# Pooling by one 144-column product per channel block, the 16 columns that reach into the next tile added by VectorE, on one TensorE-bound core

## What is computed

```python
POOL_WINDOWS = (2, 4, 8, 16)       # one for each group of 256 channels

def _pool_mixer(h_ctx, h, w_pool, pool_scale):
    he = jnp.concatenate([h_ctx, h], axis=1)
    cs = jnp.pad(jnp.cumsum(he, axis=1), ((0, 0), (1, 0), (0, 0)))
    hi = c + 1 + jnp.arange(t)
    for gi, w in enumerate(POOL_WINDOWS):
        lo = jnp.maximum(hi - w, 0)
        csg = cs[:, :, gi * 256:(gi + 1) * 256]
        mean = (csg[:, hi] - csg[:, lo]) / (hi - lo)
        ys.append(mean - h[:, :, gi * 256:(gi + 1) * 256])
    z = einsum('ntgc,gce->ntge', stack(ys), w_pool)
    return z * pool_scale
```

## Time and profile before

| | |
|---|---|
| median of three runs | 2282.36 us (2281.73 to 2285.25) |
| the profiled execution | 2281.3 us |
| its span, first to last instruction | 2279.5 us |
| PE busy in the span | 2218.8 us, 97% |
| DVE / ACT / POOL busy | 42% / 29% / 6% |
| the pooling stage, from pooling(0) to the end of the first `up_chunk` products | about 1401 to 1518 us |
| mean granted TensorE clock | 0.994 |

### The profile page before, as it was taken

One profiled execution on the slowest core, in us unless ns is written; L12 is line 12 of the kernel. 1 busy time (PEld: TensorE's weight loads), 2 busy tenths in 40 slices (PEclk: granted clock), 3 DMA queues, 4 the chain that ended last, 5 costly groups with the idle time before them and its releaser, 6 DMA issues.

```text
span 2279.5 us, 33504 instructions
## 1 busy us (share of the span) xinstructions
PE 2218.8 (97%) x13723; PEld 1996.8 (88%) x13723; DVE 961.8 (42%) x1694; ACT 658.9 (29%) x1293; POOL 137.5 (6%) x216
## 2 busy tenths in 40 slices
PE   6999999898999999999999999989999999999998
PEld 6999877686789989899898998889989899898996
DVE  4120386575643424334243345663424334243346
ACT  4111496543432203122031223451303113031121
POOL 1000130000120000000000003330000000000001
PEclk9999999999999999999999999999999999999999
DMA  5230400398321202012020123230202102021023
GB/s 167 80 86 29 158 2 2 114 404 291 102 93 46 65 10 74 27 46 64 9 74 25 49 92 110 89 102 28 66 9 74 46 28 65 9 74 45 29 90 119
DMA packets 127934, 176.15 MB, mean 77 GB/s; under 512 B 14365, under 2 KB 96469, under 8 KB 127708
## 3 DMA queue, kind: packets, MB, share of 16 engines
q1 hardware_dynamic: 121644, 170.05, 22.7%
q10 hardware_dynamic: 6192, 4.72, 0.7%
HBM read 156.40 MB, written 18.58 MB: 77 GB/s over the span
## 4 chain that ended last, share of the span: by engine, by line
PE 76%; DMA 2%; DVE 1%; SPq 1%; issue 0%; ACT 0%; POOL 0%; DVEq 0%; POOLq 0%; ACTq 0%
PE ps L1731 33%; PE ps L1711 33%; PE ps L2606 4%; DMA sa_va<-cache_a_v 1%; PE ps L2555 1%; PE ps L2574 1%; PE ps L1390 1%; PE ps L1720 1%; PE ps L1447 1%; PE ps L1410 0%; DVE m_xT_lo L2361 0%; PE ps L2626 0%; DMA sa_kb<-cache_b_k 0%; SPq L654 0%; PE ps L1430 0%
## 5 line engine op out<-in xcount | busy, mean ns | idle before, releaser
L1675 DVE TENSOR_TENSOR t_y<-t_y,ps 128x512 f32<-128x512 f32 x288 | 197.7, 687 | 626.4 <-PE ps L1731 626.2
L1731 PE MATMUL ps<-t_w_hi,t_h_hi 128*128 128x512 f32 x1152 | 449.7, 390 | 2.9 <-DVE t_h_hi L1652 2.2
L1731 PE MATMUL ps<-t_w_lo,t_h_hi 128*128 128x512 f32 x1152 | 448.4, 389 | 0.0
L1731 PE MATMUL ps<-t_w_hi,t_h_lo 128*128 128x512 f32 x1024 | 398.4, 389 | 0.0
L1711 PE MATMUL ps<-m_xT_lo,t_w_hi 128*128 128x384 f32 x1488 | 327.9, 328 | 0.0
L1711 PE MATMUL ps<-m_xT_hi,t_w_lo 128*128 128x384 f32 x1488 | 327.9, 328 | 0.0
L1711 PE MATMUL ps<-m_xT_hi,t_w_hi 128*128 128x384 f32 x1488 | 327.8, 328 | 0.0
L1606 ACT ACTIVATE t_relu<-ps 128x384 f32<-128x384 f32 (+1 forms) x192 | 87.9, 458 | 809.4 <-PE ps L1731 776.7
L1636 DVE TENSOR_TENSOR t_w_lo<-t_raw,t_w_hi 128x1024 fp32r<-128x1024 f32 x128 | 155.4, 1224 | 276.5 <-ACT t_w_hi L1594 276.1
L1731 PEld LDWEIGHTS ps<-t_w_hi,t_h_hi 128*128 128x128 f32 x1152 | 216.2, 188 | 50.9 <-DVE t_h_hi L1652 3.1
L1711 PEld LDWEIGHTS ps<-m_xT_hi,t_w_hi 128*128 128x128 f32 x1488 | 254.7, 188 | 1.1
(11 more groups left out here) (224 smaller groups left out, 2476.0 us busy)
## 6 DMA issues: line engine op xcount, KB each, us to landing
t_raw<-mlp_w SPq DMA_DIRECT2D x128, 512.0 KB, 4.0
sa_kb<-cache_b_k SPq DMA_DIRECT2D x40, 512.0 KB, 8.9
sa_vb_even<-cache_b_v SPq DMA_DIRECT2D x20, 512.0 KB, 11.3
sa_vb_odd<-cache_b_v SPq DMA_DIRECT2D x20, 512.0 KB, 10.9
in_raw<-attn_w_in SPq DMA_DIRECT2D x6, 1024.0 KB, 5.6
t_rows<-scratch_x SPq DMA_DIRECT2D x12, 512.0 KB, 5.2
qT<-x_prompt SPq DMA_DIRECT2D x8, 512.0 KB, 3.6
t_rows<-x_prompt SPq DMA_DIRECT2D x8, 512.0 KB, 3.4
```

The source lines that it names most:

```text
L1675: self.nc.vector.tensor_tensor(part, part, self.core.ps[:, 6 + n % 2, :], ALU.add).then_inc(self.part_added, 1)
L1731: mm = self.nc.tensor.matmul(self.core.ps[:, 6 + half, :], a[:, k, t * P:t * P + P], w[:, k, half * 512:(half + 1) * 512], start=(k == 0 a ...
```

## The change

Every prompt tile but the last is multiplied once for each f, by 144 columns: its own 128 and 16 more that hold its share of the next tile's first 16 positions. The last prompt tile takes 128 columns, and the sample tile stays as it was. So the 56 products of 16 columns are gone. Eight outputs of 144 columns need four banks (two to a bank), so there is one buffer, banks 0 to 3, and `pooling(q)` waits for the copy of `pooling(q - 1)` (`yT_ready` at q). ACT copies the 16 extra columns of the eight blocks to `t_carry` (128x128, seven times) ahead of its copy to `t_yT`. DVE adds them to the first 16 columns of the next tile in `t_yT` (`add_carry`, seven times), and `mix(q)` from q = 2 waits for that. `last_down` calls `during_down` after every part, and pooling(1) stands after part 10, where it stood after part 11; all other steps keep their places. Three loads of x1 rows wait for an earlier pooling step than before.

```diff
-                    pool[P + k, g, 2, j] += 1.0 / w
+                    pool[P + k, g, :, P + j] += 1.0 / w
...
-            between(p)
+                between(n)
...
-    band = core.at("t_band", XT_HI + 16 * KB, [P, 4, 3, P])
+    reach = max(POOL_W)
+    band = core.at("t_band", XT_HI + 16 * KB, [P, 4, 2, P + reach])
+    carry = core.at("t_carry", RS + 4 * KB, [P, 3, KT, reach])
...
     def pooled_ps(q):
-        return core.feature_banks(2 * (q % 2))
+        return core.banks(0, 4).rearrange("p (b c) -> p b c", b=4)[:, :, 0:2 * (P + reach)].rearrange(
+            "p b (x c) -> p b x c", x=2)
...
-            sp.wait_ge(pooled, 3)
+            sp.wait_ge(pooled, 1)
             res0.load(sp, x1, 6)
+            sp.wait_ge(pooled, 2)
             sp.wait_ge(pool_stored, 16 * NB)
             res0.load(sp, x1, 7)
-            sp.wait_ge(pooled, 4)
+            sp.wait_ge(pooled, 3)
             res0.load(sp, x1, 8)
...
                 act.wait_ge(pooled, q + 1)
                 c = columns(q)
-                nc.scalar.activation(yT[:, :, c], pooled_ps(q)[:, :, 0:c.stop - c.start], ACT.Copy).then_inc(yT_ready, 1)
+                if PLACES[q] < PT - 1:
+                    if q >= 4:
+                        act.wait_ge(carry_added, q - 3)
+                    nc.scalar.activation(by_bank(carry[:, PLACES[q] % 3]), pooled_ps(q)[:, :, :, P:P + reach], ACT.Copy)
+                nc.scalar.activation(by_bank(yT[:, :, c]), pooled_ps(q)[:, :, :, 0:c.stop - c.start], ACT.Copy).then_inc(
+                    yT_ready, 1)
...
                 elif n >= 10:
                     pool_input(n // 2 - 2)
+                    if n >= 15:
+                        add_carry(n // 2 - 5)
+
+            def add_carry(q):
+
+                t = PLACES[q]
+                first = yT[:, :, t * P:t * P + reach]
+                dve.wait_ge(yT_ready, q + 1)
+                nc.vector.tensor_tensor(first, first, carry[:, (t - 1) % 3], ALU.add).then_inc(carry_added, 1)
...
             add_z(3)
+            add_carry(6)
             add_z(4)
             next_input(3)
+            add_carry(7)
             for q in range(5, NT - 1):
                 add_z(q)
+                if q == 5:
+                    add_carry(8)
...
-                if q >= 2:
-                    pe.wait_ge(yT_ready, q - 1)
+                if q >= 1:
+                    pe.wait_ge(yT_ready, q)
...
-                    if t == 0:
-                        parts = [(x[:, fc], band[:, g, 0, :])]
-                    elif t < PT:
-
-                        parts = [(x[:, fc], band[:, g, 1, :]), (last[:, fc], band[:, g, 2, 0:reach])]
+                    if t < PT:
+                        parts = [(x[:, fc], band[:, g, int(t > 0), 0:P if t == PT - 1 else P + reach])]
...
             def mix(q):
 
                 pe.wait_ge(yT_ready, q + 1)
+                if q >= 2:
+                    pe.wait_ge(carry_added, q - 1)
...
-            def during_down(p):
-                for q in {4: (0,), 5: (1, 2), 6: (3,), 7: (4,), 8: (5,)}.get(p, ()):
+            def during_down(n):
+                for q in {9: (0,), 10: (1,), 11: (2,), 13: (3,), 15: (4,), 17: (5,)}.get(n, ()):
                     pooling(q)
-                if 5 <= p < 5 + EARLY_Z:
-                    mix(p - 5)
+                if n % 2 == 1 and 5 <= n // 2 < 5 + EARLY_Z:
+                    mix(n // 2 - 5)
```

More of the change, by code:

```diff
@@ L105, in shape_constants @@
             sample_a[NQ * h + i] = np.concatenate([window_bias(P + i - p, h), window_bias(i - new, h)])
-    pool = np.zeros((P, 4, 3, P), np.float32)
+    reach = max(POOL_W)
+    pool = np.zeros((P, 4, 2, P + reach), np.float32)
     pool_own = np.zeros((P, 4, NS), np.float32)
@@ L1913, in trunk @@
     xT_lo_done = core.sem("m1_xT_lo_done")
-    reach = max(POOL_W)
+    carry_added = core.sem("pm_carry_added")
     ALL_PARTS = NBLK * Mlp.PARTS
@@ L1921, in pooled_ps, with by_bank @@
     def pooled_ps(q):
-        return core.feature_banks(2 * (q % 2))
+        return core.banks(0, 4).rearrange("p (b c) -> p b c", b=4)[:, :, 0:2 * (P + reach)].rearrange(
+            "p b (x c) -> p b x c", x=2)
+    def by_bank(x):
+        return x.rearrange("p (b x) c -> p b x c", x=2)
     def turned_ps(q):
@@ L2024, in _ @@
             res0.load(sp, x1, 4)
-            sp.dma_start(band[:], tables["pool_band"].rearrange("p (g a c) -> p g a c", g=4, a=3)).then_inc(band_in, 16)
+            sp.dma_start(band[:], tables["pool_band"].rearrange("p (g a c) -> p g a c", g=4, a=2)).then_inc(band_in, 16)
             sp.dma_start(pool_w[:], ins["pool_w"].rearrange("(k p) n -> p k n", p=P)).then_inc(weights_in, 16)
@@ L2543, in pooling @@
                 x = res0.x(q)
-                last = res0.x(PLACES.index(t - 1)) if 0 < t < PT else None
                 for f in range(KT):
                     fc, g = slice(f * P, (f + 1) * P), f // 2
-                    if t == 0:
-                        parts = [(x[:, fc], band[:, g, 0, :])]
-                    elif t < PT:
-                        parts = [(x[:, fc], band[:, g, 1, :]), (last[:, fc], band[:, g, 2, 0:reach])]
+                    if t < PT:
+                        parts = [(x[:, fc], band[:, g, int(t > 0), 0:P if t == PT - 1 else P + reach])]
                     else:
@@ L2554, in pooling @@
                     for j, (lhs, rhs) in enumerate(parts):
-                        op = nc.tensor.matmul(pooled_ps(q)[:, f, 0:rhs.shape[-1]], lhs, rhs, start=(j == 0),
+                        op = nc.tensor.matmul(pooled_ps(q)[:, f // 2, f % 2, 0:rhs.shape[-1]], lhs, rhs, start=(j == 0),
                                               stop=(j == len(parts) - 1))
```

## The result

The changed kernel takes 2290.47 us (median of 6 runs, 2289.57 to 2294.52), the kernel before 2282.86 beside it (6 runs, 2280.85 to 2285.62). The ratio is 1.0034, with an interval of 1.0024 to 1.0045: 7.6 us slower. The forecast of 2285.3 us was wrong, and the time lies 0.5 us above the upper end of the range. The rival "the clock is low twice as long" came closest, with 2290 us. Measured by the 0.2% that the prediction set as its bound, this is slower, to which it gave 0.35.

The account below looks back on a forecast made before the run. PE, busy 97%, bounds the kernel; 11.2 us off it become three waits, with DVE's queue setting mix(5): -0.3 us. Clock terms of 1.7, 1.7 and 0.4 make +3.5: forecast 2285.3 us, range 2280.5 to 2290.

Parts of the forecast that it names:

- the clock is low twice as long: Rival: 6.8 us at half speed after each wait and dearer small operations, 8.6 us slower, 2290 us; chance 0.16.
- Steps 1 and 2: pooling(1) waits for ACT's copy of pooling(0); pooling(2) waits for the copy of pooling(1), PE idling 3.6 us.
- Step 4: mix(2) waits for add_carry(2) on DVE: PE idles 3.4 us and mix(2) starts 4.1 us later than before.
- Step 5: pooling(6) waits for ACT's copy of pooling(5): PE idles 5 us ahead of it, where it was 1.28.
- Step 6: DVE's add_z(3) sets the start of mix(5), at 1474.9 where it was 1475.43: 0.5 us gained.
- step 1: pooling(1), now ahead of part 11, waits for ACT's copy of pooling(0) until 1407.3 and takes 3.51 us.
- clock terms: Half-speed cost behind the waits ahead of pooling(2), mix(2) and pooling(6): 1.7, 1.7 and 0.4 us.
- the sum without clock: Savings, waits and DVE's queue up to mix(5) and the additions behind it, before any clock cost: -0.3 us.
- The savings arrive: Rival: ACT's copies don't hold pooling(2) and mix(2) up as worked out, 2275 to 2277 us; chance 0.06.
- Dear columns: Rival: products of 144 columns as dear as those of 256, +4.1 us on the forecast, 2289 us; chance 0.05.

Follow-up runs that it names:

- e8: The changed kernel with ACT's copies of pooling(0), (1) and (5) earlier and add_carry(2) to (5) one step earlier on DVE: 2276.33 us, ratio 0.9969.
- e5: The changed kernel with 6 and 15 products that nobody reads in PE's waits ahead of pooling(1) and pooling(2): 2286.08 us, ratio 1.0015.
- e2: The changed kernel with add_carry(2) to add_carry(5) one step earlier in DVE's sequence: 2286.93 us, ratio 1.001.
- e1: The changed kernel with pooling(1) back behind part 11: 2282.98 us, ratio 0.9995.
- e7: The changed kernel with ACT's copies of pooling(0) and pooling(1) ahead of square_y(4) and square_y(5): 2282.99 us, ratio 0.9999.
- e6: The changed kernel with pooling(1) back behind part 11 and add_carry(2) to (5) one step earlier: 2276.66 us, ratio 0.9977.
- e3: The kernel before with the 56 products of 16 columns left out and nothing added: 2275.16 us, ratio 0.9957.
- e4: The kernel before with the pooled tiles in one buffer, products and order as before: 2289.38 us, ratio 1.0022.

## Why the prediction was wrong, point by point

**The costs were right.** Pooling steps of 144 columns take 1.96 us (pooling(7), 1480.55 to 1482.51), predicted 1.95. ACT's copy of the carry takes 0.25 to 0.28 us and delays the next by 0.16 (1409.35 to 1409.51), predicted 0.24 and 0.2; DVE's addition takes 0.28, predicted 0.29:

```profile
1409.35 0.26 ACT L2142 ACTIVATE t_carry<-ps 128x128 f32<-128x128 f32 x1
1409.51 1.01 ACT L2143 ACTIVATE t_yT<-ps 128x1024 f32<-128x1024 f32 x1
...
1423.26 0.57 ACT L2143 ACTIVATE t_yT<-ps 128x512 f32<-128x512 f32 x1
```

```profile
1452.60 1.28 DVE L1505 SCALAR_TENSOR_TENSOR t_more_rows<-t_y,stats,t_raw 128x1024 f32<-128x1024 f32 x1
1453.80 0.28 DVE L2344 TENSOR_TENSOR t_yT<-t_yT,t_carry 128x128 f32<-128x128 f32 x1
```

Twice the elements cost an addition less than a third more: 128 take 0.28 us, 64 took 0.218. That agrees with the fixed price of the rule quoted in the prediction (the Trainium skill, VectorE: DVE Perf Modes, "The TRN2 errata — SBUF-src ops pay a fixed extra latency per instruction"). At seven of each they decided nothing.

**Steps 1 and 2, the wait ahead of pooling(2), right.** ACT's copy of pooling(0) ends at 1410.52, and pooling(1) starts 6.3 us after pooling(0), as worked out. PE idled 3.57 us ahead of pooling(2), predicted 3.6, and ACT's `t_yT` (1423.26, above) let it go.

**Step 4, the wait ahead of mix(2), right:** 3.30 us, predicted 3.4, let go by DVE's addition at 1453.80, which stands behind the pool input of 1452.60 (above).

**Step 5, right:** 5.00 us ahead of pooling(6), predicted 5. **Step 6, right in kind:** mix(5) was let go by DVE's `t_zn`, after a wait of 0.48 us (predicted: 1.5), and e8 shows that DVE's queue is what stands there once PE is early.

**The clock, where the forecast failed.** Its terms were 1.7, 1.7 and 0.4 us, and none for the wait of 1.46 us ahead of pooling(1).
- That wait follows from step 1 (part 10 ends at about 1405.7, pooling(1) starts at 1407.3: 1.6 us) but is left out of the clock terms and of the sentence "The 11.2 us off PE have become three waits". There are four. Behind it the clock fell for 6.8 us: pooling(1) took 5.40 us (1410.62 to 1416.02) where the prediction took over the 3.51 of before, and pooling(2) came 3.6 us later than the steps say; e5, without the fall, gets 3.2 of these back. This is the largest part that was missed. e2 repeats it: the same wait, then half speed from 1412.5 to 1419.7. That a wait so short can do it stood in the earlier trace rows: 1.28 us ahead of 1454.46 and then 6.8 us at half.
- Behind the waits ahead of pooling(2) and mix(2) the clock stayed low for 6.8 us each rather than 3.4. A part of each lies within the wait itself (1422.4 to 1423.98, 1453.1 to 1454.18), so they cost (1429.2 - 1423.98) / 2 = 2.6 and (1460.0 - 1454.18) / 2 = 2.9 us, against 1.7 each. In e5, e1 and e7 the stretch behind the wait ahead of mix(2) was only about 3.4 us long (in e5 from 1449.2 to 1452.7), as the forecast had it. So the length differs between kernels with the same wait at the same step, and this alone is worth over a microsecond.
- Around pooling(6) it cost (1477.0 - 1473.17) / 2 = 1.9, most of it taken up by slack: the lag grows by 0.9 up to mix(5), against 0.4.

Together 3.6 + 2.7 + 3.0 + 0.9 = 10.2 us in the profiled execution (last row of the table of starts, in the section on the result), where the forecast had 3.8. The medians put the clock's part nearer to 7.9 (7.6 and the 0.3 of the sum without clock). All four waits between pooling(0) and mix(5) were followed or accompanied by a fall. The rule on waits between bursts (the Trainium skill, TensorE: Matmul & The Clock Gate, "HAM oscillation — how this bites in real kernels") is borne out by the three longer ones; its example has waits longer than 1.46 us, and for one so short only the trace speaks.

**The rivals.** "Low twice as long" was right in kind, but rested on three waits at 3.4, 3.4 and 2.1; its 2290 comes near because its three prices were too high, by 0.7, 0.4 and 1.2 us, and that made up for most of the 3.6 us of the wait that it left out. "The savings arrive" was wrong for this order. e6 and e8 came into its range (2276.66 and 2276.33, by 2275 to 2277), but by a changed order, not by the queues running early that it had supposed. "Dear columns" is excluded by the 1.96 us.

**What stays open.** Which waits make the clock fall isn't settled, and neither is for how long. The length of the wait alone doesn't decide it: 2.80 us ahead of pooling(6) in e8 and 1.90 us ahead of the turn at 1499.14 in the changed kernel were followed by no fall, 1.46 us ahead of pooling(1) was. Nor does the step behind it alone. The same wait of 2.14 or 2.15 us ahead of the same turn was followed by a fall at once before, in the changed kernel, e2, e5, e6 and e8, and not in e1, e3, e4 and e7, where the clock fell 5 to 6 us later, with the next wait. And where MLP 0 begins, long ahead of the stage, the same wait of 2.37 us left the clock high before and brought it down in the changed kernel (PE's row, then the row by microsecond; before first):

```profile
665.71 0.41 PE L1720 MATMUL ps<-m_xT_hi,t_w_hi 128*128 128x320 f32 x1 [2.37 <-DVE m_xT_lo L2423]
...
668.00:669.00 1.00, 1.00 (x9) 1.00 0.86 299
```

```profile
667.46 0.41 PE L1721 MATMUL ps<-m_xT_hi,t_w_hi 128*128 128x320 f32 x1 [2.37 <-DVE m_xT_lo L2446]
...
668.00:669.00 1.00, 1.00 (x7) 0.54 0.00 0
```

So the prices of the four falls are those of one execution each. That such differences come ahead of the stage also explains why the changed kernel's profiled execution reached pooling(0) 3.3 us later than before: up to there its clock was at half for 23.8 us, against 13.6 before, in steps that the change doesn't touch. In e3, whose code up to there is that of before, it was 17.0, and pooling(0) starts at 1404.12 against 1401.02; in e7, with the code of the change, 13.6, and 1400.91. It isn't the change. Whether the short products behind the wait ahead of pooling(1) (16 pairs of 64 columns) have a part in its fall wasn't tried; in e1, e5, e6, e7 and e8 the same products ran without that wait, and no fall came.

## What to carry to other kernels

A wait on the engine that sets the pace has two prices, its own length and the clock behind it; here the clock was about half (4.4 of 8.3 us for the first two). List every new wait, the short ones too, before pricing any, and price each by the longest half-speed stretch that the trace shows behind one like it. When two buffers become one, look at what stood between the steps that share it: the cure was not in the products but in one step that had covered the copy (e1), or in the copy's place in its queue (e7), and with the additions one place earlier the change was a gain (e6).

## What the runs showed of the chip that I had not expected

- A wait of 1.46 us was followed by 6.8 us at 1.2 GHz (1412.2 to 1419), while waits of 1.69 us (before), 1.90 us (changed) and 2.80 us (e8) left the clock at 2.4 GHz. The same wait by the same code (2.37 us ahead of 665.71 and 667.46) did the one in one execution and the other in another.
- The same wait of 3.30 us ahead of mix(2) was followed or accompanied by 6.8 us of half speed in the changed kernel and by about 3.4 in e5 and e7. With one of 3.31 us ahead of pooling(6) in e4 came 10 us (1456.5 to 1466.7).
- 21 products that nobody reads, in place of two waits, made the kernel 4.4 us faster (e5 against the changed kernel).
- A record of 144 columns costs 122 ns (1.96 us for 16) beside 106 for 128 and 209 for 256.
